# First layer's modulated input: inverse norms multiplied into x ahead of the modulation vectors, its high part, scaled row and low part on three engines

## The reference

```python
def rms_norm(x, g):
    xf = x.astype(jnp.float32)
    y = xf * lax.rsqrt(jnp.mean(xf * xf, axis=-1, keepdims=True) + NORM_EPS)
    return (y * g.astype(jnp.float32)).astype(x.dtype)
...
shift, scale, gate = jnp.split(jax.nn.silu(c) @ mod_w[i] + mod_b[i], 3, axis=-1)
h = rms_norm(x, norm_g[i]) * (1.0 + scale[:, None]) + shift[:, None]
hc = rms_norm(xc, norm_g[i]) * (1.0 + scale_c) + shift_c
...
q, k, v, g = jnp.split(h @ w_in, [...], axis=-1)
```

## Time and profile before

| | |
|---|---|
| median of 3 runs | 1564.46 us (1562.63 to 1565.77) |
| the profiled execution | span 1563.3 us, 26333 instructions |
| PE busy | 1514.9 us (97%) |
| PEld | 1330.8 us (85%) |
| VectorE | 998.1 us (64%) |
| ScalarE | 812.8 us (52%) |
| GpSimd | 434.9 us (28%) |
| DMA moved | 252.24 MB, mean 161 GB/s |

### The profile page before, as it was taken

How to read it: one execution, slowest core, us unless ns; L and a number is a source line. 1 busy time by engine, 2 the same in 40 slices (tenths; PEclk the granted TensorE clock), 3 DMA queues, 4 the chain that set the end, 5 groups by cost and what they waited for, 6 DMA issues and landing times. The chain is left out here.

```text
span 1563.3 us, 26333 instructions
## 1 busy us (share of the span) xinstructions
PE 1514.9 (97%) x9520; PEld 1330.8 (85%) x9520; DVE 998.1 (64%) x2144; ACT 812.8 (52%) x1860; POOL 434.9 (28%) x507
## 2 busy tenths in 40 slices
PE   6999999999999999989999999999997999999998
PEld 3787878898889999878888888889997889999996
DVE  4655544527888888864438966665212887778783
ACT  5321221127777777755554333344112987777773
POOL 1021201001222111110012333220390564555552
PEclk9899999999999999999999999999998999999999
DMA  9444524407211155024224454479857998899882
GB/s 361 138 135 122 161 81 158 158 35 236 59 23 23 42 159 162 17 72 134 82 83 130 133 165 135 148 209 278 275 137 230 291 283 265 255 262 262 252 232 68
DMA packets 195653, 252.24 MB, mean 161 GB/s; under 512 B 32978, under 2 KB 157476, under 8 KB 195492
## 3 DMA queue, kind: packets, MB, share of 16 engines
q1 hardware_dynamic: 193076, 242.16, 51.1%
q10 hardware_dynamic: 2448, 8.39, 1.9%
HBM read 187.59 MB, written 78.76 MB: 170 GB/s over the span
## 5 line engine op out<-in xcount | busy, mean ns | idle before, releaser
L1135 ACT ACTIVATE prob<-S,nm,qk_inv 128x512 f32<-128x512 f32 (+1 forms) x208 | 146.5, 707 | 3.5 <-DVE nm L1071 3.5
L2520 DVE CUSTOM_DVE_ANT_0 nprob<-nS,bias_set 128x640 f32<-128x640 f32 x128 | 105.2, 822 | 67.4 <-PE nS L2358 45.1
L565 PE MATMUL pp<-h_hi,w_hi 128*128 128x512 f32 (+1 forms) x408 | 146.9, 360 | 0.0
L567 PE MATMUL pp<-h_hi,w_lo 128*128 128x512 f32 (+1 forms) x408 | 144.6, 354 | 0.0
L566 PE MATMUL pp<-h_lo,w_hi 128*128 128x512 f32 (+1 forms) x408 | 144.4, 354 | 0.0
L1089 DVE TENSOR_TENSOR ptlo<-TB,pthi 128x512 fp32r<-128x512 f32 (+1 forms) x192 | 114.8, 598 | 29.7 <-ACT pthi L1147 27.9
L2439 ACT CAST npt_hi<-nTB 128x256 fp32r<-128x256 f32 (+1 forms) x256 | 103.3, 426 | 56.4 <-PE nTB L2369 52.9
L1147 ACT CAST pthi<-TB 128x512 fp32r<-128x512 f32 (+1 forms) x192 | 99.4, 517 | 62.9 <-PE TB L1016 62.8
L1064 DVE TENSOR_REDUCE mx<-S 128x1 f32<-128x512 f32 (+1 forms) x208 | 116.7, 580 | 10.6 <-PE S L1008 9.3
L2533 DVE TENSOR_TENSOR npt_lo<-nTB,npt_hi 128x256 fp32r<-128x256 f32 (+1 forms) x256 | 115.1, 483 | 3.5 <-ACT npt_hi L2439 2.2
L2430 ACT ACTIVATE nprob<-nprob,selector 128x640 f32<-128x640 f32 x128 | 106.6, 832 | 12.5 <-DVE selector L2520 9.2
(11 more groups left out here) (318 smaller groups left out, 4536.2 us busy)
## 6 DMA issues: line engine op xcount, KB each, us to landing
kq_scratch<-p_stage SPq DMA_DIRECT2D x96, 256.0 KB, 3.8
keys<-kq_scratch SPq DMA_DIRECT2D x32, 768.0 KB, 4.7
bias_set<-bias_scratch SPq DMA_DIRECT2D x64, 384.0 KB, 6.4
v_strip<-v_scratch SPq DMA_DIRECT2D x128, 128.0 KB, 5.3
wearly<-in_mod_w SPq DMA_DIRECT2D x15, 1024.0 KB, 8.5
bias_scratch<-bias_wide_scratch SPq DMA_DIRECT2D x16, 768.0 KB, 10.6
w_raw<-in_na_w_in SPq DMA_DIRECT2D x11, 1024.0 KB, 6.3
wside<-in_mod_w SPq DMA_DIRECT2D x9, 1024.0 KB, 7.3
```

The costliest lines, as they stand in the source:

```text
L565: pe.matmul(acc, whi[:, k, ws], hi[:, k, a:a + width], start=(k == 0), stop=False)
L567: last = pe.matmul(acc, wlo[:, k, ws], hi[:, k, a:a + width], start=False, stop=(k == KT - 1))
L1135: act.activation(prob[:, p % 5, a:a + n], S[:, score_bank(p, k), 0:n], ACT.Exp, bias=nm[:, p % 5:p % 5 + 1], scale=q_scale(h - 1, p) if p ...
```

## The change

- `normalise` is new: VectorE multiplies block k of `xt` in place by the spread inverses, all 1280 tokens in one instruction. `spread_inverses` puts them side by side in PSUM.
- `high` replaces `high_parts`: ScalarE reads the normalised `xt`, with the scale column as its scale and the shift column as its bias, and no longer waits for the scaled row.
- `scale` moves to GpSimd and reads the normalised `xt` and the scale column only. GpSimd's queue is now: scaled row 0, first split, scaled rows 1 to 7, second split.
- `low` (VectorE) waits for both the high part and the scaled row.
- ScalarE's square-root table is loaded by a dummy root behind the first SiLU.
- VectorE's order of normalising, row copies, columns and low parts is new, and ScalarE's row copies 2 and 3 stand ahead of high parts 2 and 4 (before: 1 and 2).

```diff
@@ -169,6 +169,7 @@
         self.summed, self.rooted, self.recd, self.spread = (
             c.sem(f"{x}{l}") for x in ("summed", "rooted", "recip_done", "inv_spread"))
         self.scaled, self.his, self.los = (c.sem(f"{x}{l}") for x in ("scaled", "h_hi", "h_lo"))
+        self.normed = c.sem(f"x_normed{l}")
 
     def roots(self, act):
         act.wait_ge(self.summed, 1)
@@ -182,35 +183,40 @@
     def spread_inverses(self, pe):
         pe.wait_ge(self.recd, 1)
         for t in range(TT):
-            at = t * P + (512 - NCTX if t >= CT else 0)
+            at = 512 - NCTX + t * P
             last = pe.transpose(self.rb[:, at // 512, at % 512:at % 512 + P],
                                 self.inv[:, t:t + 1].broadcast_to([P, P]), self.consts["ident"][:, :])
         last.then_inc(self.spread, 1)
 
-    def high_parts(self, act, vectors):
-        for k in range(KT):
-            if k % 4 == 0:
-                act.wait_ge(vectors.colsd, 2 * (k // 4) + 2)
-            if k in (1, 2):
-                vectors.take_row(act, k + 1, act.copy)
-            for j, (a, n, s) in enumerate(self.PARTS):
-                act.wait_ge(self.scaled, 2 * k + j + 1)
-                act.activation(self.hi[:, k, a:a + n], self.t_[:, k % 2, a:a + n], ACT.Identity,
-                               bias=self.mod[:, self.l, k, s:s + 1]).then_inc(self.his, 1)
-
-    def scale(self, dve, k):
-        rb = self.rb.rearrange("p a n -> p (a n)")
+    def normalise(self, dve, k):
+
+        inverses = self.rb.rearrange("p a n -> p (a n)")[:, 512 - NCTX:512 - NCTX + T]
+        dve.tensor_tensor(self.xt[:, k, :], self.xt[:, k, :], inverses, ALU.mult).then_inc(self.normed, 1)
+
+    def high(self, act, vectors, k):
+        if k % 4 == 0:
+            act.wait_ge(vectors.gains, 2 * (k // 4) + 2)
+            act.wait_ge(vectors.colsd, 2 * (k // 4) + 2)
+        act.wait_ge(self.normed, k + 1)
+        for a, n, s in self.PARTS:
+            act.activation(self.hi[:, k, a:a + n], self.xt[:, k, a:a + n], ACT.Identity,
+                           bias=self.mod[:, self.l, k, s:s + 1],
+                           scale=self.mod[:, self.l, 8 + k, s:s + 1]).then_inc(self.his, 1)
+
+    def scale(self, pool, vectors, k):
+        if k % 4 == 0:
+            pool.wait_ge(vectors.gains, 2 * (k // 4) + 2)
+        pool.wait_ge(self.normed, k + 1)
         for j, (a, n, s) in enumerate(self.PARTS):
             if k >= 2:
-                dve.wait_ge(self.los, 2 * (k - 2) + j + 1)
-            dve.scalar_tensor_tensor(out=self.t_[:, k % 2, a:a + n], in0=self.xt[:, k, a:a + n],
-                                     scalar=self.mod[:, self.l, 8 + k, s:s + 1],
-                                     in1=rb[:, 512 * j:512 * j + n],
-                                     op0=ALU.mult, op1=ALU.mult).then_inc(self.scaled, 1)
+                pool.wait_ge(self.los, 2 * (k - 2) + j + 1)
+            pool.tensor_scalar(self.t_[:, k % 2, a:a + n], self.xt[:, k, a:a + n],
+                               self.mod[:, self.l, 8 + k, s:s + 1], None, ALU.mult).then_inc(self.scaled, 1)
 
     def low(self, dve, k):
         for j, (a, n, s) in enumerate(self.PARTS):
             dve.wait_ge(self.his, 2 * k + j + 1)
+            dve.wait_ge(self.scaled, 2 * k + j + 1)
             dve.scalar_tensor_tensor(out=self.lo[:, k, a:a + n], in0=self.t_[:, k % 2, a:a + n],
                                      scalar=self.mod[:, self.l, k, s:s + 1], in1=self.hi[:, k, a:a + n],
                                      op0=ALU.add, op1=ALU.subtract).then_inc(self.los, 1)
@@ -408,7 +414,7 @@
         beside = SummedVectors(c, io, mod, cols, [rb, sums], [side_sum0, side_sum1], [early[6], side1],
                                [(1, j, b) for j in range(3) for b in range(2)] + [(0, 2, 0), (0, 2, 1)], consts)
         BESIDE = len(beside.halves)
-        squared_x, turned_x = c.sem("x_squared"), c.sem("x_turned")
+        squared_x, turned_x, root_table = c.sem("x_squared"), c.sem("x_turned"), c.sem("root_table_first")
         cst, cst0 = c.sem("const_ready"), c.sem("const_zeroed")
         s_vec, s_x = c.sem("vec_loaded"), [c.sem(f"x_loaded{t}") for t in range(TT)]
         csz, lane = c.sem("silu_pad_zeroed"), c.sem("lane_sum_ready")
@@ -657,6 +663,9 @@
 
                 act.wait_ge(s_vec, 16 * 6)
                 act.activation(vec[0:16, :], vec[0:16, :], ACT.Silu).then_inc(silu, 1)
+                act.wait_ge(cst, 3)
+                act.activation(norm.root[:, 0:1], consts["eps"][:, :], ACT.Sqrt).then_inc(root_table, 1)
+                act.wait_ge(root_table, 1)
                 for t in range(TT):
                     act.wait_ge(turned_x, 2 * t + 1)
                     act.copy(xt[:, 0:4, t * P:(t + 1) * P],
@@ -667,7 +676,10 @@
                 act.wait_ge(squared_x, TT)
                 act.sem_inc(norm.summed, 1)
                 norm.roots(act)
-                norm.high_parts(act, vectors)
+                for k in range(KT):
+                    if k in (2, 4):
+                        vectors.take_row(act, k // 2 + 1, act.copy)
+                    norm.high(act, vectors, k)
 
                 act.wait_ge(gains, 1)
                 for n in range(N):
@@ -742,20 +754,22 @@
                                     tps[:, 1, :].rearrange("p (k q) -> p k q", k=4)).then_inc(taken[1], 1)
                 vectors.take_row(dve, 0, dve.tensor_copy)
                 norm.reciprocals(dve)
+                dve.wait_ge(norm.spread, 1)
+                norm.normalise(dve, 0)
                 vectors.columns(dve, 0)
+                norm.normalise(dve, 1)
+                norm.normalise(dve, 2)
                 vectors.take_row(dve, 1, dve.tensor_copy)
-                dve.wait_ge(norm.spread, 1)
-                dve.wait_ge(vectors.gains, 2)
-                norm.scale(dve, 0)
+                norm.normalise(dve, 3)
                 vectors.columns(dve, 1)
-                for k in range(1, KT):
-                    if k == 4:
-                        dve.wait_ge(vectors.gains, 4)
-                    norm.scale(dve, k)
-                    norm.low(dve, k - 1)
-                    if k in (2, 3):
-                        vectors.columns(dve, k)
-                norm.low(dve, KT - 1)
+                for k in range(4):
+                    norm.normalise(dve, k + 4)
+                    if k == 2:
+                        vectors.columns(dve, 2)
+                    norm.low(dve, k)
+                vectors.columns(dve, 3)
+                for k in range(4, KT):
+                    norm.low(dve, k)
                 dve.tensor_scalar(cols[:, 64:65], cols[:, 64:65], HD ** -0.5, None, ALU.mult).then_inc(gains, 1)
                 dve.wait_ge(tabs, 32)
                 for n in range(N):
@@ -797,7 +811,10 @@
                 pool.affine_select(out=ident[:, :], in_=ident[:, :], compare_op=ALU.not_equal, fill=1.0,
                                    base=0, pattern=[[-1, P]], channel_multiplier=1).then_inc(cst, 1)
                 pool.wait_ge(cst, 3)
+                norm.scale(pool, vectors, 0)
                 first.split(pool, 0)
+                for k in range(1, KT):
+                    norm.scale(pool, vectors, k)
                 first.split(pool, 1)
                 pool.memset(selector[:, :], 0.0).then_inc(sel_zero, 1)
                 pool.wait_ge(sel_zero, 1)
```

## The result

| | before | after |
|---|---|---|
| median of 4 runs each, same chip | 1564.09 us | 1572.92 us (1571.35 to 1574.23) |
| ratio after to before | | 1.0047, interval 1.0034 to 1.0060 |
| span of the profiled execution | 1563.3 us | 1572.4 us |

What follows compares the result with a forecast made beforehand. PE, busy 97% of the span, was taken as the bound, with one removable wait of 0.89 us for h; all else was to cost PE nothing. So 1564.46 - 0.89 = 1563.6 us, range 1560.5 to 1572.

Steps and rivals of the forecast that it cites:

- GpSimd's price: GpSimd's scaled rows: a pair of tensor_scalar, 256 and 1024 wide, per k-block was priced at 1.44 us.
- wrong if above 1.3 us for 1024: Sign on GpSimd: the forecast fails if tensor_scalar of 1024 takes above 1.3 us; near 1.04 was expected.
- The rule for the meetings: VectorE's low, with two SBUF operands, and GpSimd's instructions never overlap; normalise, with a PSUM operand, overlaps freely.
- 50.6 + 7 x 3.79: First projection stage: GpSimd's pairs and second split and VectorE's lows in series end at 50.6 + 7X, 60.7 us forecast.
- rival (a): GpSimd falls behind and tile 1 waits: 8 to 12 us slower, 1572 to 1576 us; chance 0.22.
- X = 3.09: X is the time of one GpSimd scaling pair; 3.09 us is its dear end, at the two-input subtract's rate.
- the kind of lateness foreseen: SP's queue: weights for tiles 2 and 3 land at 66.4 us; slack 1.2 us at the squares, excess falls on PE.
- The relay: PE and ScalarE alternate products, row copies and turns from 36.12 us to the first projection matmul at 46.63; forecast unchanged.
- The bound that the forecast put on any gain: First projection tile: no gain above 0.9 us unless the PE and ScalarE relay or the clock moves.
- The wait at the seventh block: PE's one wait for h in the first projection tile, before the k-block at 60.56 us; costs 0.89 us.
- Rival (b): The clock stays at 1.00 or the PE and ScalarE relay moves: 7 us faster, 1557.5 us; chance 0.07.

Runs made afterwards that it cites:

- e1: Changed kernel with GpSimd's tensor_scalar for the scaled row replaced by a copy (low parts wrong); median 1564.52 us, ratio to before 0.9988.
- e2: Changed kernel with GpSimd's tensor_scalar multiplying by the constant 1.25 in place of the scale column (low parts wrong); single run, 1570.62 us.
- e3: Changed kernel with GpSimd's scaled row made by a two-input product with the spread scale column; median 1572.51 us, ratio to before 1.0045.
- e10: Changed kernel with the scaled row made by ScalarE, GpSimd only splitting weights; median 1564.28 us, ratio to before 0.9998.
- e9: Kernel before with only the square-root table load moved behind the first SiLU; ratio to before 1.0003.
- e11: e10 plus 17 matmuls with unread results filling PE's gaps between 29 and 45 us; ratio to before 1.0002.
- e4: Changed kernel with GpSimd's second split of the weights moved ahead of scaled row 4; median 1579.66 us, ratio to before 1.0090.
- second profile: The changed kernel run and profiled once more, unaltered; median 1574.51 us, ratio to before 1.0062.
- e5: Changed kernel with all scaled rows made by VectorE, GpSimd only splitting weights; median 1566.42 us, ratio to before 1.0017.
- e6: Changed kernel with scaled rows 4 to 7 made by VectorE and 0 to 3 by GpSimd; median 1568.36 us, ratio to before 1.0010.

## Why the prediction was wrong

**The failing step is GpSimd's price.** I took 1.44 us for a pair, from the cast's rate. It measured 3.79 alone and 4.29 beside the lows; even the upper bound of 3.09, which rested on the two-input subtract, was too low. The argument "one tensor operand, so the rate of one-input work" is disproved by e1 and e2: copy and `tensor_scalar` both have one tensor operand, 1043 and 2789 ns. The one-element row of 191 ns could say nothing on the rate. The condition was written down ("wrong if above 1.3 us for 1024") and it is what happened; the mistake was to give it 0.22.

**The rule for the meetings was half right.** Whole instructions did exclude each other for the copy (a 256-wide one took 1.33 us in place of 0.40) and for the product (e3). They did not for `tensor_scalar`, which overlaps low and grows: 3.36 for 2.87 us, with the wide low at 1.43 for 1.28. The narrow low (0.47 alone) shows how: it kept its time when it began 2.0 us into a wide `tensor_scalar`, and took 1.33 us when it began 0.6 us into one. Two such meetings of after:

```profile
45.24 3.36 POOL L213 TENSOR_SCALAR scaled<-xt,mod 128x1024 f32<-128x1024 f32 x1
47.21 0.47 DVE L220 SCALAR_TENSOR_TENSOR h_lo<-scaled,mod,h_hi 128x256 fp32r<-128x256 f32 x1
...
53.73 3.36 POOL L213 TENSOR_SCALAR scaled<-xt,mod 128x1024 f32<-128x1024 f32 x1
54.30 1.33 DVE L220 SCALAR_TENSOR_TENSOR h_lo<-scaled,mod,h_hi 128x256 fp32r<-128x256 f32 x1
```

Why it is so was not tried. The Trainium skill ("SBUF — State Buffer", section on the two separate sides) says that the engine that comes second "fully blocks" for the whole instruction of the other. The traces agree for copy and two-input product, and for low with a PSUM operand, which costs GpSimd nothing (2844 ns); they differ for `tensor_scalar`. The measurement decides. By full exclusion, 50.6 + 7 x 3.79 = 77.1 us would end the split; measured 70.15, since 35.8 + 30.0 + 4.4 for the split is all there is. So two errors of opposite sign met: the pair's price was 2.6 times too low, and the exclusion too strict, and rival (a) with its X = 3.09 named the right time, 1572 to 1576, by luck: by its own rule the measured price would have given 14 us of lateness at tile 1 and not 6.

**The Trainium skill's other figure** ("GPSIMD Engine Reference", the section on performance versus the Vector engine) gave an estimated 2.3 us a pair by its 1.8 cycles per element. It pointed the right way, above 1.8 us where tile 1 begins to wait, and fell short of the 3.79 measured.

**What held.** `normalise` took 1.49 us (forecast 1.54) and started at 26.47; the table load cost nothing; the first tile began at 46.45 us at clock 0.50 (forecast 46.6); ScalarE's row copies came on time; at the squares the excess was 0.5 us, from the kind of lateness foreseen. The relay was untouched. The bound that the forecast put on any gain, 0.89 us, did not hold: e1 has tile 1 3.3 us and e10 2.1 us earlier. The wait at the seventh block was not all that stood between PE and an earlier tile 1. The clock came back at 43 to 45 us in those two profiles, about 52 in before, and the shorter chain of lows could use it. The clock alone is not enough: e9 had it back at 43 us without the shorter chain, and tile 1 stayed at 64.0. That the shorter chain alone gains less is argued, since no profile has it with a clock that returns at 52 us.

Rival (b) gave 7 us to the clock and left the chain of lows out. With the clock at 1.00 up to 46 us and a shorter chain, e11 has tile 1 only 1.6 us earlier. The medians of e1 and e10 show no measurable gain. Their profiles are of executions shorter than the median (1560.79 and 1562.89 us, medians 1564.52 and 1564.28), and an execution whose clock returns late can use the chain less; that this is what levels the medians is argued, not shown, since a median has no trace.

**The remainder.** Of +9.1 us, 6.0 are the lows and the second split, 0.5 the squares, 1.7 the order at the keys in this execution, and 0.9 spread behind. In the same code from the last stage on, the profiles range from e1's -0.9 us (-3.4 to -4.3) through after's +1.2 to e4's +7.3 (+12.7 to +20.0), with no difference in the program there. What sets that part was not tried and stays open; it is also why the last output in the table says less of the change than tile 1. It bears on medians too: of after's 8.8 us the first stage gives 6.5 (7.5 in the second profile), and the rest no profile ties to the change.

## What to carry to other kernels

- An operation that the trace does not show may cost more than the two-input work that it does show. Its upper bound has to lie above such a row, and where a whole queue rests on it, the case in which it is dear is no side case. A price for an engine goes by operation, not by the number of operands.
- Ahead of moving work to an idle engine, add up that engine's new total against the time until its last result is needed: here 30.0 + 4.4 us from 35.8, with 27.5 us to go. When the total is over, another order inside the queue need not help; the one tried here made it worse (e4).
- A wait seen in one execution bounds the gain only as long as neither the clock nor the chain beside it moves. Two near-equal bounds (relay at clock 0.50, chain of lows) have to move together: e9 moved the first alone and gained 0.2 us at tile 1, e1 and e10 had both and gained 3.3 and 2.1.
- A long wait of PE can cost twice. In the second profile of after, in e2 and in e3 the block behind a wait of 1.9 to 2.5 us ran at half the clock and cost 1.0 to 1.2 us more, and two kernels can then look alike at tile 1 that are not (e2 and after).

## What the runs showed of the hardware

- GpSimd, 1024 elements of float32 in each of 128 partitions, alone: copy 1043 ns, product with a spread column 1892, subtract of two full rows 2360, `tensor_scalar` 2870 with a column and 2789 with a constant. The multiplication by one scalar was slower than the subtract of two full rows. With a column, VectorE takes 743 ns for it (e5) and ScalarE 1136 (e10).
- The exclusion of GpSimd and VectorE differs by instruction: total for copy (256 wide: 1.33 us for 0.40) and product (1.52 for 0.61), partial for `tensor_scalar` (1024 wide: 3.36 for 2.87), none against a low with an operand in PSUM (2844 ns).
- The granted clock fell to 0.50 by about 35 us in every profile in which PE had gaps at 29 to 36 us, and not in the one where they were filled. Its return to stay varied between about 43 and 52 us, for the same program too (after: 52, second time: about 44); in e6 it was back from about 37 to 41 us and fell once more.
